# Decoder block on one core: the four buffers of the weight ring moved to four different addresses modulo 512 bytes, every other matmul operand to address 0 modulo 512

## The reference, cut to what matters

```python
h = rmsnorm(x, norm1_g) * (1 + sc1) + sh1
z = h @ w_in                                     # 2048 x 1024 by 1024 x 3584
u_conv, u_ssm, gl_conv, gl_ssm = split(z)
y_conv = conformer_conv(u_conv, ...)             # 31-tap depthwise conv, layernorm, silu, @ conv_proj
y_ssm = s5_mixer(u_ssm, ...)                     # diagonal state space in 8-step blocks, gelu, @ ssm_glu
merged = sigmoid(gl_conv) * y_conv + sigmoid(gl_ssm) * y_ssm
x = x + g1 * (merged @ w_out)
h = rmsnorm(x, norm2_g) * (1 + sc2) + sh2
f_gate, f_up = split(h @ w_ffn_in)               # 2048 x 1024 by 1024 x 5632
x = x + g2 * ((silu(f_gate) * f_up) @ w_ffn_out) # 2048 x 2816 by 2816 x 1024
out = rmsnorm(x, final_g)
```

## Time and profile before

| | |
|---|---|
| time, median of 2 runs | 2560.09 us (2556.27 and 2563.9) |
| profiled execution: span from its first to its last instruction | 2553.8 us |
| difference of span and median time | 6.3 us |
| PE busy | 2493.2 us, 98% of the span |
| POOL busy | 1749.5 us, 69% |
| DVE busy | 1699.4 us, 67% |
| ACT busy | 863.5 us, 34% |
| mean DMA rate | 155 GB/s |

### The profile page before, as it was taken

How to read it: one execution, slowest core, us unless ns; L and a number is a source line. 1 busy time by engine, 2 the same in 40 slices (tenths; PEclk the granted TensorE clock), 3 DMA queues, 4 the chain that set the end, 5 groups by cost and what they waited for, 6 DMA issues and landing times. The chain is left out here.

```text
span 2553.8 us, 31364 instructions
## 1 busy us (share of the span) xinstructions
PE 2493.2 (98%) x11419; PEld 2049.0 (80%) x11419; DVE 1699.4 (67%) x2045; ACT 863.5 (34%) x1367; POOL 1749.5 (69%) x1188
## 2 busy tenths in 40 slices
PE   7999999999999999999999999999999999999997
PEld 3778788888888888887788888878888888888886
DVE  5899748966599647977733333484565336789797
ACT  4222421143111521135433244542232334445444
POOL 2676777777776878666787776788778774445544
PEclk9999999999999999999999999999999999999999
DMA  8496347563575446573332323325666327466533
GB/s 278 149 237 190 116 160 218 137 193 112 188 198 171 149 139 200 152 232 102 115 91 84 90 75 124 101 69 151 193 179 205 96 78 242 159 215 205 185 96 120
DMA packets 426161, 395.66 MB, mean 155 GB/s; under 512 B 92232, under 2 KB 330520, under 8 KB 424472
## 3 DMA queue, kind: packets, MB, share of 16 engines
q1 hardware_dynamic: 324112, 317.83, 40.8%
q10 hardware_dynamic: 101896, 75.82, 10.0%
HBM read 317.88 MB, written 67.24 MB: 151 GB/s over the span
## 5 line engine op out<-in xcount | busy, mean ns | idle before, releaser
L2179 POOL TENSOR_TENSOR w_lo<-raw,w_hi 128x1024 fp32r<-128x1024 f32 x192 | 489.4, 2549 | 15.4
L2177 POOL CAST w_hi<-raw 128x1024 fp32r<-128x1024 f32 x192 | 216.9, 1130 | 367.0 <-PE bank L1865 266.3
L1863 PE MATMUL bank<-h_hi,w_hi 128*128 128x512 f32 x896 | 352.5, 393 | 2.0 <-ACT sg_c L1414 1.1
L1865 PE MATMUL bank<-h_hi,w_lo 128*128 128x512 f32 x896 | 349.4, 390 | 0.0
L1864 PE MATMUL bank<-h_lo,w_hi 128*128 128x512 f32 x896 | 349.3, 390 | 0.0
L829 DVE SCALAR_TENSOR_TENSOR bank<-uc,cwt,bank 128x512 f32<-128x512 f32 x464 | 323.2, 749 | 6.2
L2202 POOL TENSOR_TENSOR fw_lo<-fsum,fw_hi 128x512 fp32r<-128x512 f32 x176 | 235.6, 1342 | 74.0 <-ACT fw_hi L1573 73.8
L1863 PE MATMUL bank<-xc_hi_T,fw_hi 128*128 128x512 f32 x704 | 276.3, 392 | 5.8 <-DVE tr L1024 3.8
L1865 PE MATMUL bank<-xc_hi_T,fw_lo 128*128 128x512 f32 x704 | 274.8, 390 | 0.0
L1864 PE MATMUL bank<-xc_lo_T,fw_hi 128*128 128x512 f32 x704 | 274.5, 390 | 0.0
L2229 POOL TENSOR_TENSOR ow_lo<-raw,ow_hi 128x512 fp32r<-128x512 f32 x116 | 162.7, 1405 | 159.8 <-ACT ow_hi L1614 159.7
(11 more groups left out here) (333 smaller groups left out, 5287.7 us busy)
## 6 DMA issues: line engine op xcount, KB each, us to landing
raw<-in_w_in SPq DMA_DIRECT2D x112, 512.0 KB, 4.1
raw<-in_w_ffn_in SPq DMA_DIRECT2D x66, 512.0 KB, 6.1
hid_scratch<-tr SPq DMA_DIRECT2D x88, 256.0 KB, 3.2
raw<-tsum_scratch SPq DMA_DIRECT2D x66, 256.0 KB, 3.2
g2b<-in_w_ada SPq DMA_DIRECT2D x64, 256.0 KB, 3.9
ssm_m<-vk_scratch SPq DMA_DIRECT2D x32, 512.0 KB, 5.1
raw<-in_ssm_glu SPq DMA_DIRECT2D x32, 512.0 KB, 3.9
raw<-in_w_out SPq DMA_DIRECT2D x32, 512.0 KB, 3.7
```

Source lines behind the costliest of these rows:

```text
L1863: t.matmul(dst, wh, xh, start=first, stop=False)
L1865: return t.matmul(dst, wl, xh, start=False, stop=last)
L2177: g.tensor_copy(hi[:], src[:]).then_inc(hi_done, 1)
L2179: g.tensor_tensor(lo[:], src[:], hi[:].bitcast(F32), ALU.subtract).then_inc(split_done, 1)
```

## The change

The addresses of buffers change and nothing else: each engine's queue has the same instructions in the same order, with the same waits.

- The four halves of the weight ring no longer stand end to end. The space for them grows by 384 bytes, and they start 64, 128, 256 and 320 bytes further into it, in the order `w_hi0`, `w_hi1`, `w_lo0`, `w_lo1`. Their addresses are 13504, 17664, 21888 and 26048, residues 192, 256, 384 and 448.
- `align()` takes its residue from `h_at` (30208, residue 0) instead of `raw_at`. So `h_hi`, `h_lo`, `ys`, `yn`, `m`, `ssm_m`, the seven streamed operands `xc`, `ow`, `quarter`, `ident`, `mean_w` and the first three `fw` slots have residue 0. `raw` keeps its address and residue 128.
- `carry`, `ctmp` and `mag_t`, 128 bytes each, move behind `wst`, where the cursor was rounded up anyway.
- The `fw` slots 3 to 6, and `hid` with them, follow the ring's halves: residues 192 (slot 3), 384 (slot 4), 256 (slot 5), 448 (slot 6). A slot's high and low part have the same residue.

```diff
         def align():
-            cursor[0] += (raw_at - cursor[0]) % 512
+            cursor[0] += (h_at - cursor[0]) % 512
 
         raw_at = cursor[0]
         raw = [place(f"raw{s}", [P, CH]) for s in range(RAW)]
-        w_hi = [place(f"w_hi{s}", [P, CH], F32R) for s in range(SPL)]
-        w_lo = [place(f"w_lo{s}", [P, CH], F32R) for s in range(SPL)]
+        split_at = cursor[0]
+        w_at = [split_at + 64, split_at + 4096 + 128, split_at + 2 * 4096 + 256, split_at + 3 * 4096 + 320]
+        w_hi = [place(f"w_hi{s}", [P, CH], F32R, at=w_at[s]) for s in range(SPL)]
+        w_lo = [place(f"w_lo{s}", [P, CH], F32R, at=w_at[SPL + s]) for s in range(SPL)]
+        cursor[0] = split_at + 2 * SPL * 4096 + 384
         h_at = cursor[0]
...
         cwt = place("cwt", [P, KC, TAPS])
-        carry = place("carry", [P, G])
-        ctmp = place("ctmp", [P, G])
-        mag_t = place("mag_t", [P, G])
         mag_k = place("mag_k", [P, G, NC + 1])
...
         wst = place("wst", [P, G, NC + 1])
+        carry = place("carry", [P, G])
+        ctmp = place("ctmp", [P, G])
+        mag_t = place("mag_t", [P, G])
...
-        fw_at = [spare_at, yz_at, yz_at + 4096, raw_at + RAW * 4096, raw_at + RAW * 4096 + 8192,
-                 raw_at + RAW * 4096 + 4096, raw_at + RAW * 4096 + 12288]
+        fw_at = [spare_at, yz_at, yz_at + 4096, w_at[0], w_at[2], w_at[1], w_at[3]]
```

## The result

The changed kernel takes 2587.89 us (two runs, 2587.85 and 2587.93) against 2560.09 us before; the ratio is 1.0113, 95% interval 1.0090 to 1.0137. Run again later beside the kernel before it gave 2584.26 us against 2557.18, 1.0105 (1.0086 to 1.0124). It is slower by about 1.1%: inside the predicted range, under the 2% that the chances were about, and on the other side of "no change".

The account below looks back on a forecast made before the run. The prediction took PE's spacing of wide matmuls to bound the kernel. Its three terms of 0 left the span at 2553.8 us; with the runs' median 6.3 us above that, it forecast 2560 us, range 2538 to 2618.

Parts of the forecast that it names:

- What bounds the kernel: Whole kernel: PE busy 2493.2 of 2553.8 us, with 10152 wide matmuls at 0.2267 us making 2301 us, 90% of the span.
- The extra 0.0136 us: Each wide matmul at 2.4 GHz: cost above half its 1.2 GHz time; 138 us over 10152, the only large possible gain.
- Which matmuls change: Mixers and FFN: 7776 wide matmuls get a ring half against residue 0; the other 2376 keep equal residues.
- The price of a distance: The 7776 matmuls with differing residues: taken as 0, between 106 us less and 41 or 80 us more.
- Rival 1: Mixers and FFN: lock between load and stream lost as distance changes every third load; 41 us slower, 2601 us; chance 0.30.
- The price of 41 us: Slower case for the 7776 matmuls: 0.0053 us more each, from a mean spacing of 0.232 after a late load.
- The argument for a return within a product: FFN: a slot's two parts share one residue, so the state could be found again within a product's 12 matmuls.
- Rival 2: The 7776 matmuls: stream and load no longer meet; 2506 to 2537 us in part, 2454 wholly; chance 0.20.
- Rival 3: Memory addresses: differences in multiples of 64 bytes do not matter; 2560 us, counted within the 0.50 for no effect.
- The sentence against any effect: TensorE: the Trainium skill says its two read ports are independent and it waits for nobody; change 0, time 2560.
- The writers: POOL, DVE and ACT writing: 0 taken; PE's waits for `w_lo` under 10 us, casts and subtractions within 5%.
- The range: Whole kernel: 2538 to 2618 us, from a partial gain to past 2601, about 0.1 left out at each end.

Follow-up runs that it names:

- e1: Matmul-only kernel, sections of 60, varying distance (stationary minus streamed start address): 0.2267 us a matmul at 0, 0.2333 at 64, 0.2325 at 128, 0.2288 at 192.
- e6: Matmul-only kernel as e1, with address pairs in turn, finer equal residues and shorter streams: both at 32 took 0.2270 us, (0, 0) with (64, 64) 0.2317.
- e8: Matmul-only kernel as e1, with sections in a chosen sequence: distance 16 took 0.2267 us behind distance 0 and 0.2332 behind 64.
- e2: Changed kernel with all four ring halves put at constant distance 64: 2594.19 us against 2559.05 for the kernel before, ratio 1.0137.
- e3: Changed kernel with the ring halves put at distances 0, 256, 256 and 0: 2558.03 us against 2559.05 for the kernel before, ratio 0.9993.
- e4: Changed kernel with the change's ring distances kept in the mixers and the FFN's slots put to distance 0: 2570.94 us, ratio 1.0047 to the kernel before.
- e9: Changed kernel with all four ring halves put at constant distance 192: 2571.82 us against 2557.18 for the kernel before, ratio 1.0059.

## Why the prediction was wrong, point by point

- **What bounds the kernel: right.** PE's own spacing is the bound. Of the span's 32.3 us it brought some 27: 16.0 in the mixers (from 20.1 of spacing, with shorter gaps), 7.1 in the FFN input, 3.7 in the output. The 6.6 us around the long subtraction are the rest, less about 1 us at the two ends, and nothing shows that they belong to the change. The extra 0.0136 us was the right place to look, but no address gives it back: 0.2267 is the lowest steady spacing of fp32r at 512 columns in e1, e6 and e8.
- **Which matmuls change: right.** 7776 have a new distance, the other 2376 keep 0.2267 (slots 0, 1, 2 after). Their residue 0 instead of 128 was rightly costed at nothing.
- **The price of a distance: this step failed.** It was put at 0, and it measured 0.0048 us in the mixers and 0.0035 in the FFN. I took 0 because "two of these three rows vary just what the change varies". The earlier trace rows show one late load in a stream of equal ones, and e8 shows that a favourable state is held over: even 60 matmuls at distance 16 stay at 0.2267 if they come from it. A single event cannot show what a lasting distance does. The earlier trace rows are not fp32r and are bound by their loads, and I had said so and still counted them. The earlier trace rows are another engine. The row that was nearest to the change was the one that I kept for the rival: the earlier trace rows, a PE out of its state for ten matmuls at a mean of 0.232 us. That the mixers after have just this mean is not shown to be more than chance: it is the average of 0.2333 and 0.2308 there.
- **Rival 1: right in sign and near in price, wrong in its condition as the only one.** The loss does not need a distance that changes at every third load (e2), and a change by 256 costs nothing (e3). A constant distance has a price of its own, 0.0066 us at 64, 0.0058 at 128, 0.0022 at 192 and 0 at 256. But in the mixers more of the loss, 0.0033 of 0.0054 us, is there only when the distances follow each other (e4), as rival 1 has it or by a state held over. The price of 41 us took 0.0053 us for all 7776; the mixers' 3840 with the ring stationary had 0.0048 more than their mean before, the FFN's 3168 some 0.0035, since slots 3 and 6 are at 0.229 and slot 5 comes down to 0.2267. The changed kernel's spacing came to some 31 us in all (20.1, 7.5 and 3.7) against 41. The argument for a return within a product was wrong for slots 3, 4 and 6 and right for slot 5: it starts at over 0.23 behind slot 4 and ends at 0.2267.
- **Rival 2** (the extra goes): wrong, and so is the estimate that went with it. The Trainium skill's figure of 512 / 2.4 + 2.5 ns ("TensorE: Matmul & The Clock Gate", section "Back-to-back issue gap"), which the page gives for a single matmul and without a type, is what bf16 does here back to back, 0.2157 us, and not what fp32r does.
- **Rival 3** (a grain of 64 bytes makes all this nothing): wrong by e2.
- **The sentence against any effect.** The rule that TensorE's two read ports are independent and that it waits for nobody ("SBUF — State Buffer", section "Who interferes with whom", in the Trainium skill) agrees with the 80 us of the earlier trace rows. It says nothing of addresses, and reading it as "so an address costs nothing" was wrong: 0.2267 against 0.2333 us with no other engine at work in e1. Whether the two ports meet there, or something else takes the time, no run shows.
- **The writers: right.** Casts 1116 ns, subtractions 2568 ns, both within 2% of before; PE's loads waited for `w_lo` 3.2 us in all.
- **The range** held the time; the point and the chance of 0.50 for no effect did not. The rows showed that timing between load and stream matters by 5 to 10 ns a matmul. With that in hand, equal residues everywhere were a special case, and leaving it was likelier to cost than not. That the time fell inside the range is owed to its upper end, which was rival 1's, and not to the forecast's mechanism.

## What to carry to other kernels

With fp32r matmuls of 512 columns, keep the start addresses of stationary and streamed tiles equal modulo 256 bytes, and both on multiples of 32; some 3% of PE's time hangs on it. If tiles must differ, a mixture of distances can cost more than the constant ones do on average. A transient in the trace that ends by itself tells that the steady state is one of several: as an estimate, price a change that could end it by the transient's mean for good (here 41 us for a spacing that measured 31), and not by an event that the steady state happens to survive. A law of such a state is tested by two runs that hold the distance constant, not by more rows of the old kernel.

## What the runs showed of the hardware that was not expected

- The mean spacing of back-to-back fp32r matmuls of 128x512 at 2.4 GHz: 0.2267, 0.2333, 0.2325 and 0.2289 us at constant distances of 0, 64, 128 and 192 bytes, and the same again from 256 on (e1, stationary tile moved).
- Distances that follow each other don't cost the mean of their constant values: 0.2311 against 0.2274 us for 0, 0, 192 in turn (e1), 0.2333 against 0.2301 in the changed kernel's mixers, but 0.2267 against 0.2300 for 0 and 64 in turn with the stream moved (e6).
- Two spacings for the same distance by what stood before: 0.2267 and 0.2333 us at 16 and 272 (e8), 0.229 and 0.2333 at 192 (e9, 216 matmuls in a row).
- Fewer stationary columns can be slower: 0.2301 us with 64 columns against 0.2267 with 128, at the same address (e1); with 8 columns it is 0.2267 again (e8).
- The extra 0.0133 us is there once in a matmul of 512 or 256 columns, is halved with 256 streamed and 64 stationary columns (0.1133 us), and is absent for bf16 (0.2157 us). What takes it is not settled.
- One POOL subtraction of 6.48 us among its like of 1.27 to 1.75 us at one point of the FFN output, in four of ten profiles, costs 4.2 to 4.6 us of waiting and a stretch at a lower clock. Nine DVE instructions run beside it at 0.68 us each; in the other profiles DVE's next one waits instead (1.78 us). Why it goes one way or the other is open.
